# First mixer of two token groups in one phase with shared weight tiles

## What is computed

```python
for l in range(2):
    h = rms(x, norm_mix[l])
    if l == 0:                      # "l0" in the kernel
        q, k, v, zu, zv = split(h @ w_in_ab)          # 512, 128, 128, 512, 512 columns
        a = window_attention(rms(q), rms(k), v, rel_bias, sink)   # window 128, blocks of 128
        b = gelu(zu) * (causal_W_s @ layernorm(gelu(zv)) + b_s)   # chunks of 128
        x = x + concat(a, b) @ w_out_ab
    else:                           # "l1": HGRN2 scan, gated
        x = x + (rms_head(hgrn2(h @ w_in_c)) * sigmoid(gate)) @ w_out_c
    h = rms(x, norm_ffn[l])         # "f0", "f1"
    x = x + (silu(h @ w_gate[l]) * (h @ w_up[l])) @ w_down[l]     # d_ff = 2816
```

## Time and profile before

| | us |
|---|---|
| median of 3 runs | 1653.05 (1651.9 to 1653.59) |
| the profiled execution | 1653.56 |
| its span, slowest core | 1652.0 |
| spans of the eight cores | 1639.1 to 1652.0 |
| TensorE busy | 1585.9 |
| VectorE, ScalarE, GpSimd busy | 998.0, 619.8, 452.5 |

### The profile page before, as it was taken

One profiled execution on the slowest core, in us unless ns is written; L12 is line 12 of the kernel. 1 busy time (PEld: TensorE's weight loads), 2 busy tenths in 40 slices (PEclk: granted clock), 3 DMA queues, 4 the chain that ended last, 5 costly groups with the idle time before them and its releaser, 6 DMA issues.

```text
span 1652.0 us, 35140 instructions; the slowest of 8 cores (1639.1 to 1652.0 us)
## 1 busy us (share of the span) xinstructions
PE 1585.9 (96%) x11831; PEld 978.1 (59%) x11831; DVE 998.0 (60%) x2125; ACT 619.8 (38%) x1160; POOL 452.5 (27%) x773
## 2 busy tenths in 40 slices
PE   5899999999999999999998999999899999999998
PEld 3454446766657665566564757656564477676443
DVE  6765655765558776565545564588676477664333
ACT  3834324544236543242323342244442365422100
POOL 6342122221223223331323322243343322222110
PEclk9999999999999999999999999999899999999999
DMA  9798899969959989978799868589898756355541
GB/s 202 160 161 134 158 149 193 162 103 176 171 113 205 156 178 166 198 181 197 205 199 210 153 124 160 129 183 184 170 206 192 164 143 142 110 172 177 180 157 74
DMA packets 76526, 272.36 MB, mean 165 GB/s; under 512 B 8656, under 2 KB 10352, under 8 KB 76320
## 3 DMA queue, kind: packets, MB, share of 16 engines
q0 software_dynamic: 56800, 204.50, 65.7%
q1 hardware_dynamic: 13120, 47.74, 8.7%
q10 hardware_dynamic: 6432, 17.88, 2.9%
HBM read 374.36 MB, written 44.60 MB: 254 GB/s over the span
## 4 chain that ended last, share of the span: by engine, by line
PE 87%; DMA 6%; ACT 2%; issue 2%; DVE 2%; POOL 1%; ACTq 0%; DVEq 0%; POOLq 0%; SPq 0%
PE bank L1065 36%; PE bank L1085 18%; PE bank L790 11%; PE bank L1125 7%; PE bank L1156 3%; PE bank L1207 3%; DMA wt<-wall 2%; PE bank L781 1%; PE bank L939 1%; DMA X<-tb 1%; DMA X<-sin 1%; PE bank L1004 1%; DMA sts<-X 1%; DMA nks<-p 1%; PE bank L1019 0%
## 5 line engine op out<-in xcount | busy, mean ns | idle before, releaser
L1065 PE MATMUL bank<-hT,wt 128*128 128x264 bf16 (+3 forms) x4224 | 672.5, 315 | 4.9 <-DVE hT L784 2.3
L1065 PEld LDWEIGHTS bank<-hT,wt 128*128 128x128 bf16 x4224 | 408.4, 98 | 222.7 <-issue 10.1
L1085 PE MATMUL bank<-wt,af 128*128 128x512 bf16 x1452 | 326.0, 380 | 7.5 <-DMA wt<-wall 3.5
L649 POOL DMA_DIRECT2D wt<-wall x284 | 161.3, 570 | 614.9 <-PE bank L1065 194.2
L1069 ACT ACTIVATE ft<-bank 128x320 f32<-128x320 f32 (+3 forms) x264 | 122.4, 465 | 410.2 <-PE bank L1065 388.0
L1070 DVE SCALAR_TENSOR_TENSOR ft<-ft,bank 128x320 f32<-128x320 f32 (+3 forms) x264 | 137.2, 521 | 196.3 <-ACT ft L1069 195.6
L1085 PEld LDWEIGHTS bank<-wt,af 128*128 128x128 bf16 x1452 | 139.8, 98 | 171.5 <-issue 12.8
L1091 DVE SCALAR_TENSOR_TENSOR X<-bank,X 128x512 f32<-128x512 f32 (+1 forms) x140 | 93.1, 666 | 151.1 <-PE bank L1085 148.8
L1071 DVE TENSOR_TENSOR af<-ft,bank 128x320 bf16<-128x320 f32 (+3 forms) x264 | 137.5, 521 | 51.0 <-PE bank L1065 34.5
L662 POOL TENSOR_TENSOR st<-st,mhalf 128x1 f32<-128x1 f32 (+5 forms) x153 | 130.4, 853 | 19.5 <-DVE mask L692 0.2
L775 ACT ACTIVATE hb<-X 128x1024 bf16<-128x1024 f32 x68 | 71.8, 1057 | 153.9 <-DVE X L1091 60.1
(11 more groups left out here) (213 smaller groups left out, 1676.0 us busy)
## 6 DMA issues: line engine op xcount, KB each, us to landing
wt<-wall POOLq DMA_DIRECT2D x260, 512.0 KB, 9.5
wt<-wsc POOLq DMA_DIRECT2D x104, 512.0 KB, 6.1
wsc<-wt SPq DMA_DIRECT2D x44, 512.0 KB, 9.4
X<-xin SPq DMA_DIRECT2D x18, 512.0 KB, 10.2
wt<-wall POOLq DMA_DIRECT2D x24, 384.0 KB, 7.5
y<-X ACTq DMA_DIRECT2D x16, 512.0 KB, 8.3
X<-sin SPq DMA_DIRECT2D x16, 512.0 KB, 9.2
sts<-X ACTq DMA_DIRECT2D x16, 512.0 KB, 7.7
```

What stands on the lines that cost most here:

```text
L649: S.op("pool", lambda e: e.dma_start(out=b.ap[:, 0:cols], in_=wall[g][:, 0:cols]), w=[b], dma=b, nbytes=512 * cols, lead=lead, prio=prio)
L1065: i = e.matmul(b.ap[:, 0:n], lhsT=w.ap[:, o + k * 128:o + k * 128 + 128], rhs=hT[st.par][:, k, lo:lo + n], start=(k == 0), stop=(k == 7))
L1085: i = e.matmul(b.ap[0:n], lhsT=act[k].ap[:, st.sl(blk)], rhs=w[k // 4].ap[:, (k % 4) * 512:(k % 4) * 512 + 512], start=(k == 0), stop=(k = ...
```

## The change

Groups A and B go through l0 together in phase 0, A as stream 0 and B as stream 1. B uses A's eleven weight tiles (`early`) in place of loads of its own. Phase 1 holds f0 of A alone; phases 2 to 8 keep their content. The seven projection tiles enter FIRST, the four output tiles move there, so that all eleven are stored as bf16 in phase 0 and groups C and D read the copies.

B's mixer output gets a place of its own, aTb, which is the memory of eight of the twelve af buffers; these are lent until its last reader is done. B's five blocks are loaded with a fixed prio, gated on tile u0. In phase 0 each stream may hold three key, three value and eight p12 buffers; all buffers of a projection (`hold`) or of an attention block are granted together at its first matmul, and `qk` runs for three blocks first, for the others between the gates. Cut to its core:

```diff
@@ Sched.schedule
+                        n = sum(x.pool is b.pool for x in o.news) if len(o.news) > 1 else 1
+                        if n > 1:
+                            fr = sorted(x[0] for x in b.pool.free if x is not None)
+                            if len(fr) < n or b.pool.held.get(b.stream, 0) + n > b.cap:
+                                ok = False
+                                break
+                            f = fr[n - 1] + b.pool.margin
...
+                    if b.pool.inner is not None:
+                        for i in range(8):
+                            b.pool.inner.free[i] = b.pool.free[b.slot]
+                        b.pool.free[b.slot] = None
@@ FIRST, KEEP
-FIRST = ["%s0" % x for x in ("f", "qc", "vc", "gc")] + ["o10%d" % k for k in range(2)] + ["gu1_%d" % j for j in range(1, 21, 2)]
-KEEP = FIRST + (["o0%d%d" % (h, k) for h in range(2) for k in range(2)] + ["gu0_%d" % j for j in range(2, 22, 5)]
+FIRST = ["kv", "q0", "q1", "u0", "u1", "g0", "g1"] + ["o0%d%d" % (h, k) for h in range(2) for k in range(2)] + ["%s0" % x for x in ("f", "qc", "vc", "gc")] + ["o10%d" % k for k in range(2)] + ["gu1_%d" % j for j in range(1, 21, 2)]
+KEEP = FIRST + (["gu0_%d" % j for j in range(2, 22, 5)]
@@ build_program
+        aTb = pA.tensor[:, 0:8, :]
+        pAB = Pool("ab", [aTb])
+        pAB.inner = pA
+        for i in range(8):
+            pA.free[i] = None
...
+        def joint(st):
+            return st is stages[1] and S.key[0] == 0
@@ load_w
-                S.op("sp", lambda e: e.dma_start(out=wsc[g][:, 0:cols], in_=b.ap[:, 0:cols]), r=[b], w=[k], dma=Second(b), nbytes=256 * cols, lead=lead - 0.1)
+                S.op("sp", lambda e: e.dma_start(out=wsc[g][:, 0:cols], in_=b.ap[:, 0:cols]), r=[b], w=[k], dma=Second(b), nbytes=256 * cols, lead=lead - 0.1 if S.key[0] else -0.3)
@@ out_proj
+            aT = aTb if joint(st) else aTm
...
-                w = [load_w("%s%d%d" % (name, half, k), prio=0.06 * half + 0.03 * k + 0.15 if S.key[0] == 0 else None) for k in range(2)]
-                mark.extend(x.writer for x in w)
+                w = [early["%s%d%d" % (name, half, k)] if joint(st) else load_w("%s%d%d" % (name, half, k), prio=0.06 * half + 0.03 * k + 0.15 if S.key[0] == 0 else None) for k in range(2)]
+                if S.key[0] == 0:
+                    early.update(("%s%d%d" % (name, half, k), w[k]) for k in range(2))
@@ l0
-            w_kv, *w6 = [early[x] if st is stages[0] else load_w(x) for x in names]
+            w_kv, *w6 = [early[x] if S.key[0] == 0 else load_w(x) for x in names]
@@ qk
+                hold = []
+                if S.key[0] == 0:
+                    V65[blk], kT[blk] = pV.get("V", stream[0]), pK.get("kT", stream[0])
+                    hold += [V65[blk], kT[blk], t, sq]
+                    if full:
+                        qT[blk] = p12.get("qT", stream[0])
+                        hold.append(qT[blk])
@@ gate_v
+                if S.key[0] == 0:
+                    xh, t1 = p12.get("xh", stream[0]), p25.get("t1", stream[0])
+                    hold = [gl, xh, t1]
@@ attn
-                PT = {}
+                PT = {(g, kb): p12.get("PT", stream[0]) for g in range(2) for kb in range(2)}
+                ot = p12.get("ot", stream[0])
...
-                        S.op("pe", mm, r=[kk, qT[blk]], w=[b])
+                        o = S.op("pe", mm, r=[kk, qT[blk]] + (list(PT.values()) + [ot] if S.key[0] == 0 and g + kb == 0 else []), w=[b])
@@ l0, order of the blocks
-            for blk in allb:
-                qk(blk)
+            todo = list(allb)
+            for _ in range(3 if S.key[0] == 0 else len(allb)):
+                qk(todo.pop(0))
...
+                if blk not in todo and todo and blk == todo[0] - 1:
+                    qk(todo.pop(0))
@@ start, plan
+        for i, b in enumerate(stages[1].kv):
+            load_x(b, prio=-2.2 + 0.02 * i, gate=early["u0"].writer)
...
-        plan = [[(0, "l0", A)], [(1, "f0", A), (0, "l0", B)], [(1, "f0", B), (0, "l1", A)], [(1, "f1", A), (0, "l1", B)],
+        plan = [[(0, "l0", A), (1, "l0", B)], [(1, "f0", A)], [(1, "f0", B), (0, "l1", A)], [(1, "f1", A), (0, "l1", B)],
...
-                    if st is not A:
+                    for p in (pK, pV):
+                        p.caps = {0: 3, 1: 3} if ph == 0 else None
+                    p12.caps = {0: 8, 1: 8} if ph == 0 else None
+                    if ph:
...
-                            load_x(b, gate=first_pe(ph - 1, 0) if st is not B else mark[1])
+                            load_x(b, gate=first_pe(ph - 1, 0))
```

More of the change, by code:

```diff
@@ L31 @@
 class Buf:
-    __slots__ = ("name", "writer", "readers", "pool", "slot", "users", "done", "stream", "fin", "cap")
+    __slots__ = ("name", "writer", "readers", "pool", "slot", "users", "done", "stream", "fin", "cap", "parent")
     def __init__(self, name, pool=None, stream=0):
@@ L203, in op @@
         o.news, o.uses = [], []
-        for b in dict.fromkeys(rr + ww):
+        for b in dict.fromkeys(rr + ww + [x.parent for x in rr + ww if x.parent is not None]):
             if b.pool is not None:
@@ L561, in mkpool @@
             t = sb(name, [128, n, size], dt)
-            return Pool(name, [t[:, i, :] for i in range(n)], [mksem() for _ in range(n)] if dma else None, **kw)
+            p = Pool(name, [t[:, i, :] for i in range(n)], [mksem() for _ in range(n)] if dma else None, **kw)
+            p.tensor = t
+            return p
         pX = mkpool("X", 12, 1024, F32, dma=True, margin=0.3)
@@ L610, in build_program @@
         r_aT = {(b, half): Buf("aT%d%d" % (b, half)) for b in range(6) for half in range(2)}
+        aB = pAB.get("aB", 1)
+        r_aB = {(b, half): Buf("aB%d%d" % (b, half)) for b in range(6) for half in range(2)}
+        for x in r_aB.values():
+            x.parent = aB
+        def joint(st):
+            return st is stages[1] and S.key[0] == 0
         def ra(st, bl, half):
+            if joint(st):
+                return [r_aB[(st.body.index(b), half)] for b in bl]
             return [r_aT[(st.body.index(b), half)] for b in bl]
@@ L832, in qk @@
                 sq, t = p25.get("sq"), p12.get("qn")
-                S.op("pe", mm_tok(lambda: bk.ap[0:n, 0:256], st, blk, lambda k: w_kv.ap[:, k * 256:k * 256 + 256], hT[st.par], 8), r=[w_kv] + rh(st, [blk]), w=[bk])
+                hold = []
[5 more added lines that the diff above has]
+                        hold.append(qT[blk])
+                S.op("pe", mm_tok(lambda: bk.ap[0:n, 0:256], st, blk, lambda k: w_kv.ap[:, k * 256:k * 256 + 256], hT[st.par], 8), r=[w_kv] + rh(st, [blk]) + hold, w=[bk])
+                head = S.all[-1]
                 S.op("act", lambda e: e.activation(out=sq.ap[0:n, 512:640], in_=bk.ap[0:n, 0:128], func=AF.Square, scale=0.125), r=[bk], w=[sq])
@@ L869, in qk @@
                 S.op("pe", tr, r=[t, r_idb], w=[bt])
-                kk = kT[blk] = pK.get("kT")
+                kk = kT[blk] = kT[blk] if hold else pK.get("kT")
                 for g in range(2):
@@ L873, in qk @@
                 if full:
-                    q = qT[blk] = p12.get("qT")
+                    q = qT[blk] = qT[blk] if hold else p12.get("qT")
                     S.op(ANY, lambda e: cp(e, q.ap[:, 0:512], bt.bf[:, 0:512]), r=[bt], w=[q])
@@ L941, in gate_u @@
                         S.op("pe", mm, r=[w_u[c // 2]] + rh(st, bl), w=[b])
-                        S.op("act", lambda e, b=b, c=c, lo=lo, n=n: e.activation(out=aTm[:, 4 + c, lo:lo + n], in_=b.ap[:, 0:n], func=AF.Gelu), r=[b], w=ra(st, bl, 1))
+                        S.op("act", lambda e, b=b, c=c, lo=lo, n=n: e.activation(out=aT[:, 4 + c, lo:lo + n], in_=b.ap[:, 0:n], func=AF.Gelu), r=[b], w=ra(st, bl, 1))
             def gate_v(blk):
@@ L946, in gate_v @@
                 b, s = bank(), pS.get("gs")
[L947 to L948 removed]
+                gl = p25.get("gl", stream[0])
+                hold = []
+                if S.key[0] == 0:
+                    xh, t1 = p12.get("xh", stream[0]), p25.get("t1", stream[0])
+                    hold = [gl, xh, t1]
+                S.op("pe", mm_tok(lambda: b.ap[0:n], st, blk, lambda k: w_g[k // 4].ap[:, (k % 4) * 512:(k % 4) * 512 + 512], hT[st.par], 8), r=w_g + rh(st, [blk]) + hold, w=[b])
                 S.op("act", lambda e: e.activation(out=gl.ap[0:n, 0:512], in_=b.ap[0:n], func=AF.Gelu), r=[b], w=[gl])
@@ L972, in gate_v @@
                     S.op("pe", tr, r=[gl, r_id], w=[bt])
-                    S.op("dve", lambda e: e.tensor_tensor(out=aTm[:, 4:8, st.sl(SB)], in0=bt.ap[:, 0:64].rearrange("p (c n) -> p c n", c=4), in1=aTm[:, 4:8, st.sl(SB)], op=ALU.mult), r=[bt], w=ra(st, [SB], 1))
+                    S.op("dve", lambda e: e.tensor_tensor(out=aT[:, 4:8, st.sl(SB)], in0=bt.ap[:, 0:64].rearrange("p (c n) -> p c n", c=4), in1=aT[:, 4:8, st.sl(SB)], op=ALU.mult), r=[bt], w=ra(st, [SB], 1))
                     return
-                xh = p12.get("xh")
+                if not hold:
```

(10 more changed lines are left out.)

22 lines of the change are left out of this document (10 added, 12 removed).

## The result

The changed kernel is slower: 1662.27 us as a median of five runs (1660.88 to 1664.29) against 1653.05 us for three runs of the kernel before on the same chip (1651.9 to 1653.59); two more runs of the kernel before, 1676.73 and 1930.58 us, were in a slower state and are left out. The ratio is 1.0063 with a 95% interval of 1.0051 to 1.0075. That is 10.4 us (8.4 to 12.4; the two medians are 9.2 us apart), where 5 us of gain were forecast. The time lies just above the range, which ended at 1662.

A forecast was written before the change was run, and what follows sets the result against it. TensorE's work bounds the kernel, so only idle time can move: ceiling 11.3 us, less 2 (table), 3 (chain), 1 (alone), 1 (loads), 1 (clock) = 3.3, with chunks filling gaps 4.8; 1653.05 - 4.8 gives 1648 us, range 1640 to 1662.

The forecast's parts named there:

- What bounds the kernel: Whole span: TensorE is busy 1585.9 of 1652.0 us; the change removes no matmul and can only move idle time.
- Part 1: Start, weight loads: 11 shared f32 loads fall away, worth nothing by itself; seven added stores cost 1.65 us each on SP.
- Part 2: Start, SP's queue: B's tokens and four stores ahead of the bias table, landing about 61.5 us, bounds 46.7 and 66.
- Part 3: Start, until the table lands: A's and B's other work fills TensorE; idle 2 us taken, bounds 0 to 10.
- Part 4: Joint phase from 61.5 us: nine attention blocks as a chain; 3 us of TensorE time lost, bounds 0 and 13.
- the first rival: Joint phase: attention chain is the bound; gain gone at 9.3 us a block, at 11 us 1661; chance 25%.
- Part 5: Feed-forward A alone: loads covered, 1 us lost; up to four chunks (14 us) can start under B's mixer tail.
- Part 6: Phase 2: four projection tiles of A's second mixer no longer loaded ahead; 1 us lost, 0 to 4.
- Part 7: Start, granted clock: a stretch such as 48 to 62 us may fall again; 1 of 3.3 us given back.
- Part 8: Phases 4 and 5: 14 tiles read as bf16, landing in 6.1 us instead of 9.5; gain 0, range 0 to 2.
- The rival of the function tables: Joint phase: alternating gates and exponentials make forty ScalarE table loads in place of twelve; 1658, chance 3%.
- The estimate of 130 us for ScalarE: Joint phase: at the skill page's switch cost, ScalarE needs 130 us, ending the phase some 12 us after TensorE's bound.

The follow-up runs named there:

- experiment 2's second kernel: Changed kernel with the seven projection copies stored late and B's token loads put behind the bias table: 1.0052 of the kernel before.
- experiment 4: Changed kernel, stores late, score tiles in four af buffers instead of p12's: 1.0039 of the kernel before; with A's output-tile loads also waiting for the table: 1.0045.
- experiment 6: Four key and four value buffers per stream instead of three: 1.0055 of the kernel before in the changed kernel, 1.0004 with late stores.
- experiment 5: Changed kernel without the seven projection copies: 1.0069 of the kernel before; also the kernel before with those copies stored in phase 1: 0.9992.
- experiment 4's first kernel: Changed kernel with stores late and the score tiles in four af buffers instead of p12's: 1.0039 of the kernel before.

## Why the prediction was wrong

- **What bounds the kernel** held: busy time is the same, and the loss is idle time within 20 to 160 us (19.2 us against 8.9, the table's columns added).
- **Part 1 failed, and it carries the largest share of the error.** It put the price of the seven stores on SP's queue, as a delay of the table, and took nothing for A's own weight loads because TensorE waited for no weight before. But the earlier trace rows has a DMA share of 1.02 to 1.03 in this stretch. In a full stretch, nine stores of 1.65 us are 15 us taken from whatever else is in flight, and A's projection tiles were in flight: six stores were issued before the last tile landed at 45.4 us. It landed 6 us later, and TensorE waited 6.9 us for weights; that a load goes through GpSimd's queue and a store through SP's did not separate them. By the Trainium skill, "DMA: Bandwidth & Descriptors", section "Queues, rings and completion order", each DMA engine takes packets in turn from every queue that has work for it; the landing times here agree. Three pairs measured the stores: 0.39% in the joint plan with three buffers, 0.39% in the old plan, 0.51% with four buffers. The slowest of the seven tiles took 28.7 to 30.4 us in the four kernels with early stores and 22.9 to 25.1 in the ten without. The cover was named ("TensorE waits for no weight") and its price if it went was not worked out. That the shared loads themselves are worth nothing, as part 1 also said, held.
- **Part 2, the order on SP**, was right in kind and short in size. The table was expected at 61.5, at most 66; it was issued at 35.42 and needed 31.2, so it was there at about 67, and its exponential ran at 71.79. The 1.65 us a transfer is time of all 16 engines, and SP's queue had 40.1% of them in 0 to 60 us, which makes about 4.1 us a transfer. Most of the table's delay is the tokens': with the stores late it still needs 27.2 us, and 13.2 with the tokens behind it as well. The tokens themselves landed 18.1 to 30.0 us after issue, the first at about 49 us, where the prediction had them from 40 on, one every 4 to 5 us.
- **Part 3** took 2 us for the idle time until the table; 20 to 60 us has 11.3, where the kernel before had 4.2. Work was not present: its weights were late, then B's tokens, then the fourth and fifth blocks' projections had no key and value buffers. This is the term of the sum that parts 1 and 2 left too small.
- **Part 4, the chain.** 3 us were taken, 13 given as a bound, and 7.0 measured in 100 to 160 us, with 9.4 us a block, just past the point of 9.3 named by the first rival. Its time of 1661 is almost the one measured, but by luck: it was worked out for 11 us a block and held nothing for the stores, and at 9.4 the same working ends the chain at 150 us and gives about 1654. The chain ended late because it began at 75.20 and not at 61.5; yet beginning early does not end it early, for in experiment 2's second kernel it begins at 49.94 and its last multiplications run at 147.27 us. Of the rival's reasons, the five buffers of one pool are not borne out (experiment 4), and the three key and value buffers are (experiment 6): 7.2 us a block with four of them. VectorE's load, 86 to 90% in 100 to 140 us, is the part that I can't separate from the table's wait.
- **Part 5.** The feed-forward alone is covered (0.7 us idle in 160 to 263). The filler of up to four chunks, worth 1 to 2 us in the sum, came too late: A's last output projection ended at 134.5 us, but its norm came late in the planned order and its feed-forward began at 156.34, with one and a half chunks ahead of B's last output projection at 161.74, when almost nothing was left to fill.
- **Part 6** was right to be small: 300 to 500 us has 1.9 us idle at the median against 1.1.
- **Part 7** was right in kind. The low clock cost 1.9 us in place of 3.3 on the profiled cores, 2.5 in place of 4.0 at the median: about 1.5 us came back, where the sum kept 2.3.
- **Part 8** took 0 with a gain of 0 to 2 us. The old plan with copies gained nothing that the interval shows (0.9992, 3.8 us either way), so it can't tell 0 from 2. In the joint plan a kernel without the seven copies is 0.45% slower than one with them (experiment 5), so there they do count, by a way that stays open.
- **The rival of the function tables** fell: nine loads stand until 240 us, fewer than the twelve of before. Nothing hung on what a switch costs. The estimate of 130 us for ScalarE would have ended 13 us past the bound, not 12.

The sum put the loss at the table and the chain, and left the resource that was full, DMA, out of the terms for the very phase into which it moved eleven stores. By the runs, the 10.4 us are 6.4 for the time at which the stores are written, 3.3 for the key and value buffers (at the edge of its interval), and next to nothing for the rest of the joint phase. With both mended the kernel is level with the one before (1.0004), so the forecast gain of 4.8 us (0.9971) is missing even then. From 20 to 160 us this kernel wins back what the low clock cost, 4.0 us at the median, but its idle time is 11.0 us against 8.9: gaps have left 60 to 100 us and stand in 100 to 160. Of the joint kernels only the one with three buffers and without the table is clearly faster than the kernel before (0.9977), near the forecast. That points to the table, by its wait or by VectorE's work on it; which of the two is open.

## What to carry to other kernels

Here a transfer that was added to a stretch with a full DMA share was paid by the next load that an engine needed, on another queue: price it at bytes over the full rate, or write it later, where the share is low. A shared load is worth what TensorE waited for that load, and here that was nothing. What the pairing could win were gaps at the start, and it gave up a partner that left no gap: 100 to 160 us, with a feed-forward beside the mixer, had no idle time; with two mixers it has 7.0 us, and 2.6 with both repairs. When a buffer count ties independent work (a projection) to work that waits for something late (a table), the wait can spread; here one number in a cap was worth 0.2%, at the edge of what the interval tells.

## What the hardware showed unexpectedly

Stores on one queue lengthened loads on another: with nine of them issued before 60 us, the last projection tile took 6 us longer (22.9 to 28.9) and the three loads behind it 8 us longer at the median (28.7 to 36.8). The spans of one execution's eight cores differ by 20.8 us (1640.3 to 1661.1 in experiment 4's first kernel) with the same program, the granted clock of a core between 0.991 and 0.996; the metric takes the last of eight, so a few microseconds of idle time show less clearly in it than in the idle time by stretch.
